# Output product in split form through the gate/up ring, and two of three split products as one 512-column matmul

## The reference

```python
fn = rms_norm(h, g_ffn_pre[i])
ff = (jax.nn.silu(fn @ w_ffn_gate[i]) * (fn @ w_ffn_up[i])) @ w_ffn_down[i]      # 2048 -> 5632 -> 2048
h = h + rms_norm(ff, g_ffn_post[i])
gate = jax.nn.sigmoid(rms_norm(h, g_ple_pre[i]) @ w_ple_gate[i])
...
def peer(h, w_pq, sub_key_1, sub_key_2, u_table, v_table):     # 16384 experts, 8 heads x 16 chosen for a token
    ...
    def chunk(args):
        ht, it, gt = args
        u = u_table[it]
        a = jnp.einsum('td,tkd->tk', ht, u)
        w = jax.nn.gelu(a.astype(jnp.float32), approximate=False).astype(ht.dtype) * gt
        return jnp.einsum('tk,tkd->td', w, v_table[it])
```

## Time and profile before

| what | value |
|---|---|
| runs | 3678.5, 3679.41, 3679.45 us |
| the profiled execution | 3680.69 us, of which the span of its instructions is 3679.0 us |
| busy | TensorE 3416.0 us (93%), VectorE 1711.9 (47%), ScalarE 1112.8 (30%), GpSimd 836.4 (23%) |
| mean granted clock of TensorE | 0.968 of full speed |
| chain that ended last | TensorE 67%, GpSimd's scatters (L1979) 15% |
| DMA | 747.48 MB, 203 GB/s over the span |

### The profile page before, as it was taken

One profiled execution on the slowest core, in us unless ns is written; L12 is line 12 of the kernel. 1 busy time (PEld: TensorE's weight loads), 2 busy tenths in 40 slices (PEclk: granted clock), 3 DMA queues, 4 the chain that ended last, 5 costly groups with the idle time before them and its releaser, 6 DMA issues.

```text
span 3679.0 us, 47548 instructions
## 1 busy us (share of the span) xinstructions
PE 3416.0 (93%) x18626; PEld 2714.3 (74%) x18626; DVE 1711.9 (47%) x2025; ACT 1112.8 (30%) x1199; POOL 836.4 (23%) x535
## 2 busy tenths in 40 slices
PE   7998879999999997799979599999999899999996
PEld 6874349999974443344557599999999888888885
DVE  4233356666656402300055688633333355555555
ACT  1122134343310001100143233444444334444441
POOL 2000000000000000000000378887888710101010
PEclk9999889999999999899989799999999999999998
DMA  7432647777769834366205246666666576666663
GB/s 254 147 120 98 216 151 273 267 264 270 264 250 345 309 137 177 107 238 254 103 36 183 77 153 208 203 205 205 206 205 205 173 256 239 245 239 241 243 238 121
DMA packets 190502, 747.48 MB, mean 203 GB/s; under 512 B 53424, under 2 KB 53456, under 8 KB 123872
## 3 DMA queue, kind: packets, MB, share of 16 engines
q1 hardware_dynamic: 125664, 664.84, 50.7%
q0 software_dynamic: 55552, 64.91, 6.5%
q10 hardware_dynamic: 9216, 16.78, 1.2%
HBM read 710.62 MB, written 35.83 MB: 203 GB/s over the span
## 4 chain that ended last, share of the span: by engine, by line
PE 67%; POOL 16%; DVE 8%; issue 4%; DMA 3%; ACT 2%; POOLq 0%; DVEq 0%; ACTq 0%; SPq 0%
POOL weight_dram L1979 15%; PE bank L410 14%; PE bank L556 12%; PE bank L557 12%; PE bank L558 12%; PE bank L394 7%; PE bank L854 5%; DMA misc<-in_w_ada 2%; DVE misc L1516 1%; DMA weight_dram<-misc 1%; PE bank L459 1%; PE bank L347 1%; DVE aux L1803 0%; POOL part_lo L1959 0%; PE bank L818 0%
## 5 line engine op out<-in xcount | busy, mean ns | idle before, releaser
L1767 DVE TENSOR_TENSOR part_lo<-ring,part_hi 128x2048 fp32r<-128x2048 f32 x248 | 568.3, 2293 | 638.6 <-ACT part_hi L1271 619.0
L556 PE MATMUL bank<-h_hi,part_hi 128*128 128x256 f32 x2304 | 656.6, 285 | 14.5 <-DVE part_lo L1767 9.0
L557 PE MATMUL bank<-h_lo,part_hi 128*128 128x256 f32 x2304 | 654.3, 284 | 0.0
L558 PE MATMUL bank<-h_hi,part_lo 128*128 128x256 f32 x2304 | 654.1, 284 | 0.0
L1271 ACT ACTIVATE part_hi<-ring 128x2048 fp32r<-128x2048 f32 x252 | 482.3, 1914 | 546.2 <-PE bank L558 544.6
L1979 POOL DMA_INDIRECT weight_dram<-misc x256 | 585.1, 2286 | 98.2 <-issue 91.9
L410 PE MATMUL bank<-ring,xT 128*128 128x512 f32 (+1 forms) x1216 | 506.8, 579 | 8.0 <-DVE xT L1466 6.3
L556 PEld LDWEIGHTS bank<-h_hi,part_hi 128*128 128x128 f32 x2304 | 444.8, 193 | 16.2 <-issue 8.7
L557 PEld LDWEIGHTS bank<-h_lo,part_hi 128*128 128x128 f32 x2304 | 444.9, 193 | 0.0
L558 PEld LDWEIGHTS bank<-h_hi,part_lo 128*128 128x128 f32 x2304 | 444.7, 193 | 0.0
L410 PEld LDWEIGHTS bank<-ring,xT 128*128 128x128 f32 x1216 | 226.8, 191 | 286.0 <-issue 285.1
(11 more groups left out here) (301 smaller groups left out, 3678.0 us busy)
## 6 DMA issues: line engine op xcount, KB each, us to landing
ring<-in_u_table SPq DMA_DIRECT2D x128, 1024.0 KB, 4.9
ring<-in_v_table SPq DMA_DIRECT2D x128, 1024.0 KB, 4.8
ring<-in_stream SPq DMA_DIRECT2D x114, 1024.0 KB, 4.8
misc<-in_w_ada SPq DMA_DIRECT2D x192, 512.0 KB, 5.6
ring<-in_gateup SPq DMA_DIRECT2D x88, 1024.0 KB, 4.8
ring<-in_down SPq DMA_DIRECT2D x16, 2816.0 KB, 11.5
ring<-in_wo_pq SPq DMA_DIRECT2D x32, 1024.0 KB, 4.8
weight_dram<-conv_tmp POOLq DMA_DIRECT2D x1, 16384.0 KB
```

What stands on the lines that cost most here:

```text
L556: nc.tensor.matmul(out, hi, x_hi, start=start, stop=False)
L557: nc.tensor.matmul(out, hi, x_lo, start=False, stop=False)
L558: return nc.tensor.matmul(out, lo, x_hi, start=False, stop=stop)
L1767: v.tensor_tensor(part_lo[j % PARTS], raw[j % RAW], part_hi[j % PARTS].bitcast(F32), ALU.subtract).then_inc(sem("lo_ready"), 1)
```

## The change

- `paired_products` replaces `split_products` in gate/up and in the dots from block 24. The hi weights meet hi and lo of the activations in one 512-column matmul: its operand is an access pattern with two runs of 256, `gap` apart (`beside`). The second matmul adds lo by hi to the right half of the bank. VectorE sums the two halves (`summed`, `dots_summed`) before silu, product and gelu.
- The output product is a split product. Its 44 chunks of 1 MB go through the gate/up ring; the lo part is written over the raw chunk; the hidden activations are split four blocks at a time into `hid_parts`, which lie over the `w_ada` slots. Outputs go by halves of the columns, the first four to banks 4 to 7.
- Modulation groups 14 to 23 leave gate/up's last round and the output product. They are done beside `pgate` (four), `lat` (two) and `qk2` (four), with their loads in between.
- `choice_exp(1)` comes one loop round later on ScalarE; the first `coefficients_hi` comes behind the last four splits and gelus.

```diff
+        def beside(name, over, lo_over, lo_first):
+            gap = (place[lo_over] - place[over]) // 4 + lo_first
+            both = rounded(name, over, 0, gap + KD * S)
...
+            def pair(k):
+                at = both[:, k * S:(k + 1) * S]
+                return bass.AP(tensor=at.tensor, offset=at.offset, ap=[list(at.ap[0]), [gap, 2], [1, S]])
...
+        def paired_products(out, hi, lo, x_hi, x_pair, start, stop):
+            nc.tensor.matmul(out[:, 0:2 * S], hi, x_pair, start=start, stop=False)
+            return nc.tensor.matmul(out[:, S:2 * S], lo, x_hi, start=False, stop=stop)
+        def halves(ps):
+            return ps[:, 0:2 * S].rearrange("p (a s) -> p s a", a=2)
...
@@ SyncE
-            sp_.wait_ge(sem("lo_ready"), 2 * KF - 1)
-            load_big(0)
...
+            for m in range(DOWN):
+                if m < RAW:
+                    sp_.wait_ge(sem("lo_ready"), SPLIT_DOWN - RAW + m + 1)
+                else:
+                    sp_.wait_ge(multiplied, gu_end + m - RAW + 1)
+                sp_.dma_start(ffn_raw[m % RAW], io["down"][m]).then_inc(raw_loaded[m % RAW], 16)
...
+            ada_some(0, 4)
+            rest("pgate", 6, 2)
+            ada_some(4, 4)
+            for j in range(8):
+                rest("pgate", 8 + j, 1)
+                ada_some(8 + 3 * j, 3)
             rest("lat", 0, 8)
+            ada_some(32, 3)
             rest("kr", 0, 1)
-            stream("qk2", 16)
+            ada_some(35, 3)
+            for j in range(16):
+                rest("qk2", j, 1)
+                ada_some(38 + 3 * j, 3)
@@ TensorE
-                        m = split_products(out_bank("gateup", j)[:, 0:S], ffn_hi[j % PARTS][:, ks], ffn_lo[j % 2][:, ks],
-                                           h3_hi[:, k, :], h3_lo[:, k, :], k == 0, k == KD - 1)
+                        m = paired_products(out_bank("gateup", j), ffn_hi[j % PARTS][:, ks], ffn_lo[j % 2][:, ks],
+                                            h3_hi[:, k, :], h3_pair(k), k == 0, k == KD - 1)
...
+            pe.wait_ge(sem("mod_ready"), ADA_FFN)
+            for m in range(DOWN):
+                half, q, c = m // (2 * HID_Q), m // 2 % HID_Q, 2 * (m // (2 * HID_Q)) + m % 2
+                pe.wait_ge(sem("lo_ready"), SPLIT_DOWN + m + 1)
+                pe.wait_ge(sem("hid_ready"), half * HID_Q + q + 1)
...
+                for k in range(4):
+                    ks = slice(k * BAND, (k + 1) * BAND)
+                    for t in range(T):
+                        ts = slice(t * P, (t + 1) * P)
+                        i = split_products(down_bank(2 * c + t)[:, :], parts[:, 0, k, ts], parts[:, 1, k, ts],
+                                           ffn_hi[m % PARTS][:, ks], down_lo[m % RAW][:, ks],
+                                           q == 0 and k == 0, q == HID_Q - 1 and k == 3)
+                i.then_inc(multiplied, 1)
...
                     product_n(pe, "pgate", 4 * c, 2 * c, 4, 4, x_lhs, it=it, per_out=4)
+                    ada_sum(ADA_FFN + 2 * it + c)
...
                 product_n(pe, "lat", 4 * c, 2 * c, 4, 4, x_lhs)
+                ada_sum(ADA_W2 + c)
             product_n(pe, "kr", 0, 0, 1, KD, x_lhs, width=64)
-            with loop(pe, 2) as it:
-                for c in range(2):
-                    product_n(pe, "qk2", 4 * c, 2 * c, 4, 4, x_lhs, it=it, per_out=4)
+            for c in range(4):
+                ada_sum(ADA_W2 + 2 + c)
+                product_n(pe, "qk2", 4 * c, 2 * c, 4, 4, x_lhs)
...
+            with loop(pe, (NEB - POOL_LOW) // PARTS) as it:
+                for j in range(PARTS):
+                    dots_of_block(j + POOL_LOW, it, paired=True)
@@ ScalarE
+            def down_upper(m):
+                a.wait_ge(raw_loaded[m % RAW], 16 * ((SPLIT_DOWN + m) // RAW + 1))
+                wait_multiplied(a, "down", m - PARTS)
+                a.activation(ffn_hi[m % PARTS], ffn_raw[m % RAW], ACT.Copy).then_inc(sem("hi_ready"), 1)
+            def hidden_hi(n):
+                if n >= 2:
+                    wait_multiplied(a, "down", 2 * (n - 2) + 1)
...
-            with loop(a, POOL_LOW // PARTS - 2) as it:
+            with loop(a, POOL_LOW // PARTS - 1) as it:
                 for j in range(PARTS):
                     upper(2 * PARTS + j, it)
                     gelu(PARTS + j, it)
             choice_exp(1)
...
-            coefficients_hi(0, first=True)
             for j in range(PARTS):
                 upper(NEB + j)
                 gelu(NEB - PARTS + j)
+            coefficients_hi(0, first=True)
@@ VectorE
+            def summed(c, it):
+                wait_multiplied(v, "gateup", c, it, 8)
+                ps = out_bank("gateup", c)
+                if c % 2 == 0:
+                    v.wait_ge(taken, out_no("gateup", 0) + c - 2 + it * 8)
+                    v.tensor_reduce(silu_g[:, c // 2 % 2, :], halves(ps), AXX, ALU.add).then_inc(
+                        sem("gate_summed"), 1)
+                else:
+                    link(v.tensor_reduce(up_sum[:, c // 2 % 2, :], halves(ps), AXX, ALU.add))
...
+            def down_lower(m):
+                v.wait_ge(sem("hi_ready"), SPLIT_DOWN + m + 1)
+                v.tensor_tensor(down_lo[m % RAW], ffn_raw[m % RAW], ffn_hi[m % PARTS].bitcast(F32), ALU.subtract)\
+                    .then_inc(sem("lo_ready"), 1)
+            def hidden_lo(n):
...
             for c in range(4):
+                ada_group(ADA_FFN + c)
...
+            ada_group(ADA_W2)
+            ada_group(ADA_W2 + 1)
             v.wait_ge(taken, out_no("kr", 0))
...
+            for g in range(ADA_W2 + 2, ADA_G):
+                ada_group(g)
             turn_out(nc.vector, "n6", 2 * KL, lambda k: latT[:, k, :], gain("g_q_lat"))
...
+            def dots_summed(j, it=0):
+                v.wait_ge(sem("expert_used"), j + 1 + PARTS * it)
+                v.wait_ge(sem("gelu_done"), j - 1 + PARTS * it)
+                v.tensor_reduce(dot_sum[:, j % 2, :], halves(bank[j % 4]), AXX, ALU.add).then_inc(
+                    sem("dots_summed"), 1)
+            for j in range(PARTS - 1):
+                lower(POOL_LOW + j)
+            with loop(v, (NEB - POOL_LOW) // PARTS - 1) as it:
+                for j in range(PARTS):
+                    lower(POOL_LOW + PARTS - 1 + j, it)
+                    dots_summed(POOL_LOW + j, it)
```

More of the change, by code:

```diff
@@ L50 @@
 SLOTS = 8
-BCH = 11 * BAND
-BSLOTS = 2
+DOWN = KF
+HID_Q = KF // 4
 ADA_W = 512
@@ L287, in out_bank, with down_bank @@
             return bank[out_no(phase, o) % 4]
+        def down_bank(o):
+            return bank[out_no("down", o) % 4 + (4 if o < 4 else 0)]
         def wait_bank(pe, phase, o, it=0, per=0):
@@ L723, in rest, with ada_some @@
                     load(phase, j)
-            rest("pgate", 6, 10)
+            def ada_some(first, n):
+                for i in range(first, min(first + n, 8 * (ADA_G - ADA_FFN))):
+                    ada_load(i % 8, ADA_FFN + i // 8)
+            ada_some(0, 4)
[4 more added lines that the diff above has]
+                ada_some(8 + 3 * j, 3)
             rest("lat", 0, 8)
+            ada_some(32, 3)
             rest("kr", 0, 1)
-            stream("qk2", 16)
+            ada_some(35, 3)
+            for j in range(16):
+                rest("qk2", j, 1)
+                ada_some(38 + 3 * j, 3)
             stream("v2", 8)
@@ L843, in _ @@
                 gateup_round(it + 1)
[L845 to L860, removed]
+            pe.wait_ge(sem("mod_ready"), ADA_FFN)
[3 more added lines that the diff above has]
+                pe.wait_ge(sem("hid_ready"), half * HID_Q + q + 1)
+                if q == 0 and half:
+                    pe.wait_ge(taken, out_no("down", 0))
+                parts = hid_parts[(half * HID_Q + q) % 2]
+                for k in range(4):
[6 more added lines that the diff above has]
+                i.then_inc(multiplied, 1)
             for c in range(4):
@@ L970, in _, with dots_of_block @@
             pe.wait_ge(taken, out_no("pq", 16))
-            def dots_of_block(j, it, first=False):
+            def dots_of_block(j, it, first=False, paired=False):
                 pe.wait_ge(sem("lo_ready"), SPLIT_EXP + j + 1 + PARTS * it)
@@ L1303, in _ @@
             choice_exp(1)
-            done = POOL_LOW // PARTS - 2
+            done = POOL_LOW // PARTS - 1
             with loop(a, NEB // PARTS - 2 - done) as it:
@@ L1574, in _, with ada_group @@
             gateup_round(0, first=True)
-            with steps.loop(KF // 4 - 2, 0) as it:
+            with steps.loop(KF // 4 - 2, 4) as it:
                 gateup_round(it + 1)
             gateup_round(KF // 4 - 1, last=True)
-            ada_row(ADA_FFN - 1)
-            for g in range(ADA_FFN, ADA_G):
+            for m in range(2, DOWN):
+                down_lower(m)
+                if m % 2 and 2 <= (m + 1) // 2 < 2 * HID_Q:
+                    hidden_lo((m + 1) // 2)
+            def ada_group(g):
                 for k in range(KD):
@@ L1916, in _ @@
```

(5 more changed lines are left out.)

146 lines of the change are left out of this document (91 added, 55 removed).

## The result

The changed kernel took 3602.01 us (median; single executions 3595.88 to 3603.56) beside 3678.97 us for the kernel before: a ratio of 0.9788, with a 95% interval from 0.9777 to 0.98. The forecast was 3601. The profiled execution took 3603.56 us with a span of 3602.0, 77.0 less than the span before.

The account below looks back on a forecast made before the run. TensorE was taken as the bound, with GpSimd's scatters beside it in the dots; 18.8 + 77.6 - 29.3 + 11 = 78.1 us off 3680.7 gave 3602.6, as a median 3601, range 3583 to 3632.

Parts of the forecast that it names:

- 1. Gate/up, paired: Gate/up stage: one 512- plus one 256-column matmul per k-step saves 0.0133 us, 18.8 us off in all.
- 2. Output product: FFN output product in split form: 1056 matmuls of 512 columns take 239.4 us, 77.6 us off, no stall charged.
- 3. What is moved: Ten modulation groups moved: 10.3 us of sums, a 16.5 us hole before block two's q/k, 2.5 for clock; 29.3 back.
- 4. Dots: Dot products from block 24: 22.2 us off TensorE, but scatters and late exponential leave 11 us off together.
- the scatters' term: GpSimd beside the shorter dot blocks: seven to nine scatters lost at 1.84 us, 13 to 17 us, taken as 15.
- The end of the scatters: GpSimd's last scatter, and with it the first coefficients: -18.3 - 1.8 + 15 = -5 us.
- The other order of the coefficients: Before the values: last splits and gelus go ahead of the coefficients, leaving 4.5 us instead of 10.3, so -5.8.
- The late exponential: Second half's exponential moved behind block 23's activation: TensorE restarts at block 24 2.7 us later, 3 with the clock.
- 3588: First rival, dots: scatters keep up, none lost, so TensorE's own path decides and gives 24.5 instead of 11; 17%.
- the smaller hole: Block two's q/k: lower bound of TensorE's hole, 14.9 us without any wait for a load, against 16.5.
- 3627: Second rival: pairing saves nothing, the fixed 0.0133 us belonging to the columns' two runs; 52.9 us off in all; 15%.
- the larger one: Block two's q/k: upper bound of TensorE's hole, 20 us with all loads in line, against 16.5.

Follow-up runs that it names:

- the changed kernel's second profile: The changed kernel run once more with no edit, beside three others of its group; 3598.31 us, ratio 0.9786.
- all edits: Changed kernel with row sums behind products, earlier second-choice exponential, low parts in two instructions, first coefficients between the last sums; 3569.03 us, again 3559.38 us.

## Why the prediction was right, step by step

**1. Gate/up, paired: right.** 18.8 us forecast, 18.9 against a profile that has the pair at 0.3467 throughout. In the profile of the result the stage gave only 16.7 (first to last matmul 503.6 us for 520.4), and the step of 0.3533 in 16 chunks is 1.7 us of the rest. The prediction had one value for all pairs. The Trainium skill (TensorE: Matmul & The Clock Gate, Back-to-back issue gap) gives a warm matmul by itself some 2.5 ns of fixed time, and says that this is too little at few columns where a weight load goes with each matmul. The trace does not agree with the 2.5 ns: the rows here have 13.3 ns, before, after and with the pairing undone, and the measurement decides. The new reductions (0.69 us) never ended a wait of TensorE in the gate/up stage.

**2. Output product: right.** 239.4 us forecast and 239.4 measured; in 1043 to 1284 us TensorE is busy without a gap, at 0.2267 us a matmul. With gate/up the two stages gave 94.4 us, forecast 96.4. No run puts the plain fp32 product back; the gain is read from the stage alone.

**3. What is moved: right.** 29.3 us forecast, 30.6 measured (4.4 + 21.3 + 4.9), with a hole of 17.02 for 16.5 and the clock at its lower level for 4.7 us behind it. The cause is shown: the sum put behind its product takes 16 us off. So 16 of these 29 us came with the place of one line, and not with the moved work.

**4. Dots: the sum right, but the scatters' term right in kind and not in size, so that luck has a part.** Forecast 11 us off from block 23 to the first value, measured 11.0 in the profile of the result, but 15.8 in the second one (601.0 us for 605.8 there, 616.8 before, counted from block 23's last matmul). The end of the scatters was put at -5 and came at -5.4 in the first, -12.9 in the second. The term behind it is the 15 us for seven to nine scatters lost. When VectorE began the last low part of the dots, 8 scatters were left before, 14 in the first profile, 10 in the second, and 12 in two variants (gate/up without pairing; the row sums behind). So the mechanism holds, since the scatters came forward by less than the dots, which gained 17.4 us; but of the 13 us (15 less the one scatter more) that the prediction takes from the dots' gain, the scatters took 11.1, 3.7 and, in the variants, 7.4. The hole ahead of the values, put at 15 to 24 us, was 17.6, then 12.8, and 13.8 in those two variants. The other order of the coefficients gave 5.8 as forecast (4.54 us from the first coefficients to the first value, 10.3 before). The late exponential was put at 2.7 us and moved TensorE's restart by 3.5; that it then also holds back the scatters' end ("the late exponential puts it 3 back") no run bears out: made early, it moved TensorE's last dot by 8.3 us and the first value by at most 4.2, which is inside the scatters' own variation of 7 us. The bound itself, the scatters, is shown from three sides: fewer of them, or shorter waits for them, bring the hole to 6.5 us; and longer dots give back only part.

**What no step had.** From the second block's transposes to block 23 the kernel was 4.7 us faster. In the second block's attention TensorE's granted clock was 1.00 where it had been 0.94 before, in the same work (58.3 and 61.1 us). Two variants that left this stage alone had 59.8 and 59.9 us, and all others, the changed kernel's second profile among them, had 58.3. So this stretch can vary while its code stays as it is, and with one profile of the kernel before it can't be told whether the change has a part in it. In total the profile of the result came 77.2 us earlier to the first value, forecast 78.1: the forecast steps fell 3.3 us short (94.4 for 96.4, 30.6 for 29.3, 11.0 for 11), the stretches that no step had gave 4.7 and took 2.3. The close hit owes that to luck; the second profile of the same kernel took 11 us less.

**Its range.** 3588 less the 1.6 us of the smaller hole is 3586, and 3627 with 3.5 us for the larger one is 3630; the stated 3583 and 3632 are a little wider than their terms. Nothing hangs on it.

## What to carry to other kernels

A row sum, or any other small consumer, goes behind the large product that can cover its producer, not in front of it: its place was worth 16 us here. Where an engine with a backlog runs beside the matmuls and the next stage waits for it, a gain on TensorE counts in full only when the backlog is gone (11 to 16 of 22 us here); look for what holds each of its instructions up, since cutting VectorE's long instruction in two shortened the chain of scatters by 150 us, for 0.07 us more of VectorE a block. And an edit that is worth nothing today is to be tried again when the bound has moved.

## What the runs showed of the hardware

- A scatter that GpSimd starts while VectorE makes a low part in SBUF waits for the end of that instruction, and ends 1.42 us behind it (3.4 us for 1.54). It slips in between two instructions of 1.2 us that follow on each other at once: in the rows above, the scatter of 2410.36 waits for the first one's end and then runs beside the second. VectorE's sum out of an accumulator bank doesn't hold one off: in the changed kernel's profile 93 scatters began during such a sum, and none took more than 1.57 us. One of them:

```profile
2406.48 0.69 DVE L1951 TENSOR_REDUCE misc<-bank 128x256 f32<-128x512 f32 x1 [1.30 <-PE bank L588]
```

```profile
2406.53 1.57 POOL L2107 DMA_INDIRECT weight_dram<-misc  x1 [0.78 <-POOL misc L2102]
```

- The same program had TensorE's pairs 0.3533 us apart for the whole of the dots in one profiled execution, and 0.3467 in the next, at a granted clock of 1.00 in both. The stage took 9.7 us more. In gate/up the longer step stood in 16 chunks in four profiles, in 8 chunks in four, and nowhere in four, always in whole rounds of 8 near the stage's start; the changed kernel has it in 16 in one profile and in 8 in the other. Where three matmuls take the pair's place, the step was 0.3600 in all chunks and blocks. Whether the operand in two runs has to do with it is not shown. It may be part of why the changed kernel's executions lie up to 11 us apart; no run shows that.
- How TensorE's clock stood behind a wait ahead of block 24: after 2.57 and 2.63 us of idle time it stayed at its upper level of 2.4 GHz in two profiles (early exponential; all edits). In the second profile of all edits, after the same 2.57 us, it fell behind the restart: from 2246 to 2248 us, 1.3 us after it, 0.50 was granted. After 4.64 us (kernel before) and 8.1 us (changed kernel) the matmuls began at 0.50. So a wait of that length can go either way in the same program.
